# FFN-in units of a hybrid decoder layer: five pairs of weight tiles in seven-product form instead of four

## The chip, the core and the metric

The kernel runs on one core of a Trainium2 chip. The metric is the device time of one execution in microseconds (us), the median of three runs. Lower is better.

## What is computed

One decoder layer on 256 tokens of width 2048, in float32: x = x + 1/2 SwiGLU_1(RMSNorm(x)), then a token mixer (16 heads of 128, half dilated-window attention, half forgetting attention), then x = x + 1/2 SwiGLU_2(RMSNorm(x)). The change touches the first product of both SwiGLU blocks:

```python
D_FF = ((8 * D_MODEL // 3 + 127) // 128) * 128     # 5504

def swiglu_ffn(x, w_in, w_out):
    gate, up = jnp.split(x @ w_in, 2, axis=-1)
    return (jax.nn.silu(gate) * up) @ w_out
```

x is 256 x 2048 here, w_in is 2048 x 11008. With D_MODEL = 2048 the weights of both FFNs are most of what the kernel reads.

## The kernel before, in words

**Products.** Each float32 value is cut into a high and a low part, and a product of two tiles is three matmuls: high x high, high x low, low x high. ScalarE makes the high part of a weight tile (`whi`, helper `split` at L849), VectorE subtracts it to get the low part (`wlo`, L1188). A "half" is what one such split gives: up to 1024 elements per partition, two weight tiles of 128 x 512. `whi` and `wlo` have `SLOTS` = 4 slots each and halves are numbered through the whole program: half h goes to slot h % 4, ScalarE waits with `weights_used` until TensorE is through with half h - 4, VectorE waits for ScalarE (`weights_hi`), TensorE for VectorE (`weights_lo`).

**Units.** FFN-in is cut into 11 units of 512 columns of gate and of up (the last one has 384). Unit 0 is plain (`plain_unit`). Units 1 to 10 (`unit`, once per engine) do contraction tiles 0 to 7 plainly and tiles 8 to 15 in a seven-product form (after Strassen and Winograd). The four blocks of weights are B11 (tiles 8 to 11, up), B12 (8 to 11, gate), B21 (12 to 15, up) and B22 (12 to 15, gate); the two blocks of tokens stand for the rows. A form is a run of two halves, and each of the weight tiles in it is multiplied for one block of tokens only: 6 matmuls a half. A plain half is multiplied for both: 12 matmuls. The order, the same on all engines, is T1, B11, (turn of the activations of the unit before), G0 (two plain halves), T2, B21, T3, G1 (two), B22, T4, U0 and U1 (four): 22 halves. T1, T2, T3 and T4 are sums of weight blocks. T1 = B11 + B12 is made by VectorE in `tsum` (`sum_t1`, L1350), T3 = B12 + B22 in place of B12 (`sum_t3`, L1357), both at the end of the unit before. T2 and T4 are made in `tsum` by accumulating transfers that POOL issues (`add_piece`, L478).

**The order of VectorE inside a unit** is written out by hand (`unit` in the vector block): the low parts in the order above, and between them SwiGLU of the unit before (three steps, L1242 to L1248, behind B11's first half), the subtraction behind G1 (L1413), the add onto the gate inside T4 (L1419), the second subtraction behind the first half of U0 (L1424), `sum_t1` behind U1's first half and `sum_t3` behind its second. It waits in this order, strictly:

```python
split(base + B11, piece_half(n + LOAD["B11"], 0, w2), w2)
swiglu(u, j - 1)
split(base + B11 + 1, piece_half(n + LOAD["B11"], 1, w2), w2)
```

**Loads.** SP issues one transfer of 1 MB per weight piece into the six slots of `raw` (`piece`, L370), each behind a wait for the last use of its slot; the eight pieces of a unit go in one order (`LOAD`). x (2 MB) stays in SBUF all the time. It is needed for the squares of its norm and then when FFN-out's result is added to it (`join`, `x_update`).

Of the kernel before, what the change touches and what calls it, by code (L numbers as in the profile page):

```python
# [43 lines left out]
T1, B11, G0, T2, B21, T3, G1, B22, T4, U0, U1 = 0, 2, 4, 6, 8, 10, 12, 14, 16, 18, 20  # L44
UNIT_HALVES = 22

LOAD = {"B11": 0, "B12": 1, "B22": 2, "G0": 3, "B21": 4, "G1": 5, "U0": 6, "U1": 7}
# [61 lines left out]
OUT_P[0] = 8 * UNITS  # L109
# [3 lines left out]
OUT_P[1] = IN_P[1] + 8 * UNITS  # L113
# [14 lines left out]

def raw_slot(n):
    for u, end in ((0, QKV_P), (1, END_P)):  # L130
        if OUT_P[u] <= n < end:
            c, i = (n - OUT_P[u]) // ACT_PAIRS, (n - OUT_P[u]) % ACT_PAIRS
            q = OUT_LOADS[c][i] - 2 * OUT_GROUPS[c]
            return 3 + (2 * c * OUT_GROUPS[0] + OUT_LOADS[c][i]) % 3 if q < 0 else (c * ACT_PLAIN[0] + q) % 3
    for first, slots in ((IN_P[1], RAW_SLOTS), (QKV_P, QKV_RAW_SLOTS), (0, RAW_SLOTS)):
        if n >= first:
            return (n - first + (sum(ACT_PLAIN) if slots == QKV_RAW_SLOTS else 0)) % slots
# [3 lines left out]
for _n in range(END_P):  # L141
    RAW_FULL[_n] = 16 * (1 + sum(1 for _m in range(_n) if raw_slot(_m) == raw_slot(_n)))
# [11 lines left out]
def layer(nc, io, out):  # L154
# [3 lines left out]
    with ctx:  # L158
# [47 lines left out]
        place[0] = arena + 36 * 1024  # L206
        xg = sb("xg", [P, KT // 2, SEQ])
# [40 lines left out]
        rows_dram = nc.dram_tensor("forget_rows", (H_B, SEQ), f32).ap()  # L248
        scratch = nc.dram_tensor("bias_vectors", (P, H_A * VEC), f32).ap()
# [23 lines left out]
        raw_full = [sem(f"raw_full{s}") for s in range(RAW_SLOTS)]  # L273
# [49 lines left out]
        xg_ready, s_summed, s_hi, s_ready = (sem(n) for n in ("xg_ready", "s_summed", "s_hi", "s_ready"))  # L323
# [19 lines left out]
        def _(sp):  # L343
            def free(n):
                for u in range(2):
                    if IN_P[u] <= n < OUT_P[u]:
                        j, i = (n - IN_P[u]) // 8, (n - IN_P[u]) % 8
                        if j == 0:
                            return weights_lo, IN[u] + 2 * i + 2
                        if i == LOAD["B21"]:  # L350
                            return t4_added, 16 * ((UNITS - 1) * u + j)
                        last = {LOAD["B11"]: B11, LOAD["B21"]: B21, LOAD["B12"]: T3, LOAD["B22"]: B22, LOAD["G0"]: G0, LOAD["G1"]: G1, LOAD["U0"]: U0, LOAD["U1"]: U1}[i]
                        return weights_lo, unit_half(u, j) + last + 2
# [9 lines left out]

            def piece(n, src, tiles, w):
                slot = raw_slot(n)
                before = [m for m in range(n) if raw_slot(m) == slot]
                if before:
                    sem_free, value = free(before[-1])
                    sp.wait_ge(sem_free, value)
                sp.dma_start(raw[:, slot, 0:tiles * w].rearrange("p (k f) -> p k f", k=tiles), src).then_inc(raw_full[slot], 16)  # L370
# [8 lines left out]
            for u in range(2):  # L379
                w_in = io[f"ffn{u + 1}_w_in"][0].rearrange("(k p) f -> p k f", p=P)  # L380
                w_out = io[f"ffn{u + 1}_w_out"][0].rearrange("(t p) d -> p t d", p=P)
                for j in range(UNITS):
                    n, w = IN_P[u] + 8 * j, UNIT_W[j]
                    gate, up = slice(W * j, W * j + w), slice(D_FF + W * j, D_FF + W * j + w)
                    if j == 0:
# [23 lines left out]
                        for q in range(4):  # L409
                            piece(n + 4 + q, w_in[:, 4 * q:4 * q + 4, up], 4, w)  # L410
                            if u == 0 and q < 2:
                                for c in (2 * q, 2 * q + 1):
                                    sp.dma_start(x[:, :, c * W:(c + 1) * W], x_rows[:, :, c * W:(c + 1) * W]).then_inc(x_loaded[c], 16)
                    else:
                        piece(n + LOAD["B11"], w_in[:, 8:12, up], 4, w)
                        piece(n + LOAD["B12"], w_in[:, 8:12, gate], 4, w)
                        piece(n + LOAD["B22"], w_in[:, 12:16, gate], 4, w)
                        piece(n + LOAD["G0"], w_in[:, 0:4, gate], 4, w)
                        piece(n + LOAD["B21"], w_in[:, 12:16, up], 4, w)
                        piece(n + LOAD["G1"], w_in[:, 4:8, gate], 4, w)  # L420
                        piece(n + LOAD["U0"], w_in[:, 0:4, up], 4, w)
                        piece(n + LOAD["U1"], w_in[:, 4:8, up], 4, w)
# [27 lines left out]
        def _(pool):  # L450
# [22 lines left out]
            def add_piece(u, j, name, after, done):  # L473
                n, w = IN_P[u] + 8 * j, UNIT_W[j]
                k, col = {"B22": (12, W * j), "B21": (12, D_FF + W * j)}[name]
                pool.wait_ge(weights_lo, unit_half(u, j) + after + 2)
                pool.wait_ge(raw_full[raw_slot(n + LOAD[name])], RAW_FULL[n + LOAD[name]])
                pool.dma_start(tsum[:, 0:4 * w], raw[:, raw_slot(n + LOAD[name]), 0:4 * w], accum_op=ALU.add).then_inc(done, 16)  # L478

            for j in range(1, UNITS):  # L480
                add_piece(0, j, "B22", T1, t2_added)
                add_piece(0, j, "B21", T2, t4_added)
            pool.wait_ge(weights_lo, out_half(0, PASSES - 1, ("form", OUT_GROUPS[1] - 1, "T4")) + 1)
# [23 lines left out]
            x_power(2)  # L507
            for j in range(1, UNITS):
                add_piece(1, j, "B22", T1, t2_added)
                add_piece(1, j, "B21", T2, t4_added)  # L510

        @block.tensor
        def _(pe):
# [45 lines left out]
            def form(h, bank_out, stationary, w, start):  # L559
                for i in range(2):  # L560
                    pe.wait_ge(weights_lo, h + i + 1)
                    slot = (h + i) % SLOTS
                    for k in range(2):
# [4 lines left out]
                        last = mm(bank_out[:, 0:w], st_lo, hi, start=False, stop=i == 1 and k == 1, skip_group_check=True)  # L568
# [32 lines left out]
            def unit(u, j):  # L601
# [3 lines left out]
                if j == 1:  # L605
                    pe.wait_ge(silu_done, 2 * (UNITS * u + 1))
                    pe.wait_ge(s_ready, 4 * (u + 1))
                    if u == 0:
# [3 lines left out]
                form(base + T1, Z, lambda k, t: sf[:, 0, k, t, :], w, True)  # L612
                form(base + B11, Y, lambda k, t: xs[:, 8 + k, t, blk0], w, True)
                act_turn(u, j - 1)
                pe.wait_ge(copied, 3 * first + 1)
                for i in range(2):
                    plain(base + G0 + i, 2 * i, (Z, X), (False, True), w, -1)
                pe.wait_ge(copied, 3 * first + 2)
                form(base + T2, Y, lambda k, t: sf[:, 1, k, t, :], w, False)
                form(base + B21, V, lambda k, t: xs[:, 12 + k, t, blk0], w, True)  # L620
                pe.wait_ge(copied, 3 * first + 3)
                form(base + T3, Y, lambda k, t: sf[:, 2, k, t, :], w, False)
                for i in range(2):
                    plain(base + G1 + i, 4 + 2 * i, (Z, X), (False, False), w, 7)
                form(base + B22, Z, lambda k, t: sf[:, 3, k, t, :], w, False)
                pe.wait_ge(w_done, first + 1)
                form(base + T4, Y, lambda k, t: xs[:, 12 + k, t, blk1], w, False)
                for i in range(4):
                    plain(base + U0 + i, 2 * i, (V, Y), (False, False), w, 7)
# [210 lines left out]
        def _(act_e):  # L840
# [58 lines left out]
            def act_hi(u, c, k):  # L899
# [6 lines left out]
                else:  # L906
                    act_e.wait_ge(weights_used, unit_half(u, UNITS - 1) + B22 + 2)
                A(aw_hi[:, a, a_in, :], act[:, k, :], ACT.Copy).then_inc(aw_hi_ready, 1)

            def group_act_hi(u, c, g, part):  # L910
# [3 lines left out]
                else:  # L914
                    act_e.wait_ge(weights_used, unit_half(u, UNITS - 1) + B22 + 2)
# [22 lines left out]
            def plain_unit(u):  # L938
                w2 = 2 * UNIT_W[0]
                for i in range(2 * IN_HALVES):  # L940
# [32 lines left out]
                    if i == 13:  # L973
                        for f in range(4):
                            act_e.wait_ge(s_summed, 4 * u + (1, 3, 3, 4)[f])
                            A(sf[:, f, :, 0, :], s_sum(f), ACT.Copy).then_inc(s_hi, 1)
                    if i == 14:
                        silu(u, 0)

            def unit(u, j):  # L980
                Y, V, Z, X = unit_banks(j)
                base, n, w, s = unit_half(u, j), IN_P[u] + 8 * j, UNIT_W[j], j % 2
                first, w2 = (UNITS - 1) * u + j - 1, 2 * w
                act_e.wait_ge(sums_done, 2 * first + 1)
                for i in range(2):
                    split(base + T1 + i, tsum[:, i * w2:(i + 1) * w2], w2)
                loaded(n + LOAD["B11"])
                for i in range(2):
                    split(base + B11 + i, piece_half(n + LOAD["B11"], i, w2), w2)
                loaded(n + LOAD["G0"])  # L990
                split(base + G0, piece_half(n + LOAD["G0"], 0, w2), w2)
                act_e.wait_ge(weights_used, base + T1 + 2)
                A(gset[:, s, 1, 0:w], Z[:, 0:w], ACT.Copy).then_inc(copied, 1)
                split(base + G0 + 1, piece_half(n + LOAD["G0"], 1, w2), w2)
                act_e.wait_ge(weights_used, base + B11 + 2)
                act_e.wait_ge(act_f_done, 2 * (UNITS * u + j))
                A(p1s[:, 0:w], Y[:, 0:w], ACT.Copy).then_inc(copied, 1)
                act_e.wait_ge(t2_added, 16 * (first + 1))
                for i in range(2):
                    split(base + T2 + i, tsum[:, i * w2:(i + 1) * w2], w2)  # L1000
                loaded(n + LOAD["B21"])
                for i in range(2):
                    split(base + B21 + i, piece_half(n + LOAD["B21"], i, w2), w2)
                act_e.wait_ge(sums_done, 2 * first + 2)
                split(base + T3, piece_half(n + LOAD["B12"], 0, w2), w2)
                act_e.wait_ge(weights_used, base + T2 + 2)
                A(gset[:, s, 0, 0:w], Y[:, 0:w], ACT.Copy).then_inc(copied, 1)
                split(base + T3 + 1, piece_half(n + LOAD["B12"], 1, w2), w2)
# [675 lines left out]
```

## Time and profile before

| what | value |
|---|---|
| median of three runs | 1764.4 us (1764.1 to 1764.69) |
| the profiled execution's own time | 1763.82 us |
| its span, first to last instruction | 1762.0 us |
| TensorE busy | 1755.3 us (100%) |
| VectorE busy | 1408.5 us (80%) |
| ScalarE busy | 1074.9 us (61%) |
| read from HBM | 347 MB, 199 GB/s over the span |
| mean granted TensorE clock | 1.000 |

Busy time of TensorE is that of pipelined matmuls whose ends are modelled: a matmul of 512 columns is shown with 0.39 us, but the next one starts 0.23 us behind it. The starts give the pace. A small gap does not lower the busy time by its length.

### The profile page before, as it was taken

What the parts mean: (1) busy time and instruction counts of PE and PEld (TensorE: products, weight loads), DVE (VectorE), ACT (ScalarE), POOL (GpSimd) and SP (SyncE); (2) the same over time, 40 slices, a digit from 0 to 9 for tenths busy, and PEclk for the clock granted to TensorE, in tenths of its full rate; (3) what the DMA queues carried; (4) which work ended last, traced back from release to release, by engine and by line L of the source; (5) the groups of instructions that cost most, each with busy time, mean ns of one, the idle gap of its engine ahead of it and who ended that gap; (6) DMA issues with size and microseconds to landing.
All of it is one profiled execution on the core that took longest, in us unless ns stands there. A gap on an engine that the chain in (4) does not pass through costs nothing.

```text
span 1762.0 us, 20916 instructions
## 1 busy us (share of the span) xinstructions
PE 1755.3 (100%) x8036; PEld 1463.3 (83%) x8036; DVE 1408.5 (80%) x1587; ACT 1074.9 (61%) x1359; POOL 62.7 (4%) x74
## 2 busy tenths in 40 slices
PE   9999999999999999999999999999999999999999
PEld 7788888888988888888888888888888888988887
DVE  7888888887899998575655655888888888799998
ACT  7566666666666666554545544666666666666665
POOL 0000000000000001100000000000000000000000
PEclk9999999999999999999999999999999999999999
DMA  9888788876654556555455547687788887764762
GB/s 378 272 261 260 251 250 249 252 252 201 217 215 184 210 215 208 178 193 177 160 188 163 173 168 262 169 256 244 249 260 260 260 261 240 226 204 166 259 213 90
DMA packets 160691, 391.75 MB, mean 222 GB/s; under 512 B 6504, under 2 KB 15232, under 8 KB 155856
## 3 DMA queue, kind: packets, MB, share of 16 engines
q1 hardware_dynamic: 152288, 342.02, 54.7%
q0 software_dynamic: 7184, 46.42, 12.6%
q10 hardware_dynamic: 1120, 1.97, 0.3%
q8 instruction: 64, 1.05, 0.2%
q14 instruction: 35, 0.29, 0.0%
HBM read 347.37 MB, written 3.69 MB: 199 GB/s over the span
## 4 chain that ended last, share of the span: by engine, by line
PE 95%; DVE 2%; DMA 1%; SPq 1%; issue 1%; ACT 0%; POOL 0%; ACTq 0%; POOLq 0%; DVEq 0%
PE bank L584 9%; PE bank L582 9%; PE bank L583 9%; PE bank L566 7%; PE bank L568 7%; PE bank L567 7%; PE bank L523 7%; PE bank L525 7%; PE bank L524 6%; PE bank L653 5%; PE bank L655 5%; PE bank L654 5%; PE bank L679 3%; PE bank L681 3%; PE bank L680 3%; PE bank L551 1%
## 5 line engine op out<-in xcount | busy, mean ns | idle before, releaser
L1188 DVE TENSOR_TENSOR wlo<-raw,whi 128x1024 fp32r<-128x1024 f32 (+1 forms) x586 | 696.6, 1207 | 224.7 <-ACT whi L849 222.0
L849 ACT ACTIVATE whi<-raw 128x1024 fp32r<-128x1024 f32 (+1 forms) x586 | 611.0, 1047 | 390.2 <-PE bank L525 189.2
L582 PE MATMUL bank<-whi,xs 128*128 128x512 f32 (+1 forms) x768 | 297.9, 388 | 0.4 <-DVE xs L1370 0.2
L584 PE MATMUL bank<-whi,xs 128*128 128x512 f32 (+1 forms) x768 | 295.6, 385 | 0.0
L583 PE MATMUL bank<-wlo,xs 128*128 128x512 f32 (+1 forms) x768 | 295.5, 385 | 0.0
L1188 DVE TENSOR_TENSOR wlo<-tsum,whi 128x1024 fp32r<-128x1024 f32 (+1 forms) x120 | 140.2, 1196 | 60.5 <-ACT whi L849 60.5
L849 ACT ACTIVATE whi<-tsum 128x1024 fp32r<-128x1024 f32 (+1 forms) x120 | 122.2, 1036 | 103.9 <-PE bank L584 64.1
L582 PEld LDWEIGHTS bank<-whi,xs 128*128 128x128 f32 x768 | 144.4, 188 | 29.0 <-issue 0.9
L584 PEld LDWEIGHTS bank<-whi,xs 128*128 128x128 f32 x768 | 144.3, 188 | 27.7
L583 PEld LDWEIGHTS bank<-wlo,xs 128*128 128x128 f32 x768 | 144.4, 188 | 26.8
L653 PE MATMUL bank<-whi,aw_hi 128*128 128x512 f32 x420 | 164.0, 391 | 0.0
L655 PE MATMUL bank<-whi,aw_lo 128*128 128x512 f32 x420 | 163.5, 389 | 0.0
L654 PE MATMUL bank<-wlo,aw_hi 128*128 128x512 f32 x420 | 163.4, 389 | 0.0
L523 PE MATMUL bank<-whi,xs 128*128 128x512 f32 x384 | 155.1, 404 | 0.4 <-DVE wlo L1188 0.4
L525 PE MATMUL bank<-whi,xs 128*128 128x512 f32 x384 | 150.1, 391 | 0.0
L524 PE MATMUL bank<-wlo,xs 128*128 128x512 f32 x384 | 149.5, 389 | 0.0
L566 PE MATMUL bank<-whi,sf 128*128 128x512 f32 (+1 forms) x320 | 122.8, 384 | 1.0 <-DVE wlo L1188 1.0
L568 PE MATMUL bank<-whi,sf 128*128 128x512 f32 (+1 forms) x320 | 122.8, 384 | 0.0
L567 PE MATMUL bank<-wlo,sf 128*128 128x512 f32 (+1 forms) x320 | 122.7, 384 | 0.0
L1052 ACT ACTIVATE whi<-raw 128x1024 fp32r<-128x1024 f32 x80 | 84.8, 1060 | 61.8 <-PE bank L655 38.9
L1453 DVE TENSOR_TENSOR wlo<-raw,whi 128x1024 fp32r<-128x1024 f32 x80 | 97.2, 1221 | 1.7 <-ACT whi L1052 0.8
L653 PEld LDWEIGHTS bank<-whi,aw_hi 128*128 128x128 f32 x420 | 78.8, 188 | 17.4 <-issue 1.4
(203 smaller groups left out, 2670.4 us busy)
## 6 DMA issues: line engine op xcount, KB each, us to landing
raw<-ffn_w_in SPq DMA_DIRECT2D x158, 1024.0 KB, 7.1
raw<-ffn_w_out SPq DMA_DIRECT2D x84, 1024.0 KB, 6.5
raw<-w_in SPq DMA_DIRECT2D x48, 1024.0 KB, 5.1
tsum<-raw POOLq DMA_DIRECT2D x36, 1024.0 KB, 7.2
raw<-w_out SPq DMA_DIRECT2D x16, 1024.0 KB, 4.9
raw<-ffn_w_in SPq DMA_DIRECT2D x16, 768.0 KB, 4.6
tsum<-raw POOLq DMA_DIRECT2D x4, 768.0 KB, 5.7
x<-x SPq DMA_DIRECT2D x4, 512.0 KB, 12.4
```

Of the source, the lines that this page charges most:

```text
L523: mm(banks[b][:, 0:w], stationary[:, k, 0, tok], hi, start=k == 0, stop=False, skip_group_check=True)
L524: mm(banks[b][:, 0:w], stationary[:, k, 0, tok], lo, start=False, stop=False, skip_group_check=True)
L525: last = mm(banks[b][:, 0:w], stationary[:, k, 1, tok], hi, start=False, stop=k == k_total - 1, skip_group_check=True)
L566: mm(bank_out[:, 0:w], st_hi, hi, start=start and i == 0 and k == 0, stop=False, skip_group_check=True)
L582: mm(banks[b][:, 0:w], xs[:, k + i, 0, tok], hi, start=starts[b] and k + i == 0, stop=False, skip_group_check=True)
L583: mm(banks[b][:, 0:w], xs[:, k + i, 0, tok], lo, start=False, stop=False, skip_group_check=True)
L584: last = mm(banks[b][:, 0:w], xs[:, k + i, 1, tok], hi, start=False, stop=k + i == last_k, skip_group_check=True)
L653: mm(bank_out[:], st_hi, hi, start=i == 0, stop=False, skip_group_check=True)
L654: mm(bank_out[:], st_hi, lo, start=False, stop=False, skip_group_check=True)
L655: last = mm(bank_out[:], st_lo, hi, start=False, stop=k == FT - 1, skip_group_check=True)
L849: A(whi[:, h % SLOTS, 0:n_el], src, ACT.Copy).then_inc(weights_hi, 1)
L1188: V.tensor_tensor(wlo[:, h % SLOTS, 0:n_el], src, whi[:, h % SLOTS, 0:n_el].bitcast(f32), ALU.subtract).then_inc(weights_lo, 1)
```

## The change

Tiles 6 to 15 go through the seven-product form (five pairs) and tiles 0 to 5 are plain. Each form has three halves, of two, two and one weight tiles (15 matmuls), and the six plain halves are GA, GB, GC and UA, UB, UC. A unit has 27 halves. `SLOTS` stays 4. The fifth tile of each block (a "mini", 256 KB) is a transfer of its own, and so is its part of the accumulating transfers; VectorE's two sums get a second instruction of 512 elements each. The minis and one plain piece lie in SBUF where x was: in FFN 1 x is loaded for its squares and again behind the units, in FFN 2 POOL stores it to DRAM (`x_kept`) and loads it again. SP's queue waits in unit 1 for that (`ss_done`, `x_psum`, `x_stored`). There are five slots for form pieces and three for plain half pieces, and SP's order of loads is a new one. `sum_t3` moves from the end of the unit before to between GA and GB of its own unit; `sum_t1` of the next unit stands between UA and UB. The forms' token sums (`form_sums`) are of five tiles, with one more split (`last_form_split`).

```diff
-T1, B11, G0, T2, B21, T3, G1, B22, T4, U0, U1 = 0, 2, 4, 6, 8, 10, 12, 14, 16, 18, 20
-UNIT_HALVES = 22
+FORM_K0, FORM_PAIRS = 6, 5
+T1, B11, GA, GB, T2, B21, T3, GC, B22, T4, UA, UB, UC = 0, 3, 6, 7, 8, 11, 14, 17, 18, 21, 24, 25, 26
+UNIT_HALVES = 27
...
+            def form_piece(u, j, name):
...
+                wait_free(n)
+                sp.dma_start(raw[:, raw_slot(n), 0:4 * w].rearrange("p (k f) -> p k f", k=4),
+                             w_in[:, k:k + 4, col:col + w]).then_inc(raw_full[raw_slot(n)], 16)
+                if j == 1 and name == "B11":
+                    sp.wait_ge(ss_done, 8 * (2 * u + 1))
+                    if u:
+                        sp.wait_ge(x_psum, 8)
+                        sp.wait_ge(x_stored, 16)
+                sp.dma_start(minis[:, raw_slot(n), 0:w], w_in[:, k + 4, col:col + w]).then_inc(raw_full[raw_slot(n)], 16)
...
                     else:
+                        if j + 1 < UNITS:
+                            form_piece(u, j + 1, "B12")
+                        plain_piece(u, j, "UA")
+                        plain_piece(u, j, "UB")
+                        if j + 1 < UNITS:
+                            form_piece(u, j + 1, "B22")
+                        plain_piece(u, j, "UC")
+                        if j + 1 < UNITS:
+                            form_piece(u, j + 1, "B21")
+                            if j + 2 < UNITS:
+                                form_piece(u, j + 2, "B11")
+                            plain_piece(u, j + 1, "GA")
+                            plain_piece(u, j + 1, "GB")
+                            plain_piece(u, j + 1, "GC")
...
             def add_piece(u, j, name, after, done):
+                pool.dma_start(tsum[:, 0:4 * w], raw[:, raw_slot(n), 0:4 * w], accum_op=ALU.add).then_inc(done, 16)
+                pool.dma_start(tmini[:, 0:w], minis[:, raw_slot(n), 0:w], accum_op=ALU.add).then_inc(done, 16)
+
+            def x_again(u):
+                pool.wait_ge(weights_lo, OUT[u])
+                pool.dma_start(x[:], (x_kept if u else io["x"][0]).rearrange("(b p) d -> p b d", p=P)).then_inc(x_back, 16)
...
             def unit(u, j):
-                for i in range(2):
-                    split(base + T1 + i, tsum[:, i * w2:(i + 1) * w2], w2)
-                split(base + B11, piece_half(n + LOAD["B11"], 0, w2), w2)
+                for i in range(3):
+                    form_split(T1, i)
+                form_split(B11, 0, "B11")
                 swiglu(u, j - 1)
-                split(base + B11 + 1, piece_half(n + LOAD["B11"], 1, w2), w2)
-                split(base + G0, piece_half(n + LOAD["G0"], 0, w2), w2)
-                split(base + G0 + 1, piece_half(n + LOAD["G0"], 1, w2), w2)
+                for i in range(1, 3):
+                    form_split(B11, i, "B11")
+                plain_split("GA", GA)
+                sum_t3(u, j)
+                plain_split("GB", GB)
...
+                for i in range(3):
+                    form_split(B22, i, "B22")
+                form_split(T4, 0)
+                dve.wait_ge(weights_used, base + GC + 1)
                 dve.wait_ge(w_done, first + 1)
                 V.tensor_tensor(gset[:, s, 1, 0:w], X[:, 0:w], gset[:, s, 1, 0:w], ALU.add).then_inc(gate_added, 1)
-                split(base + T4 + 1, tsum[:, w2:2 * w2], w2)
-                split(base + U0, piece_half(n + LOAD["U0"], 0, w2), w2)
-                dve.wait_ge(weights_used, base + B22 + 2)
+                for i in range(1, 3):
+                    form_split(T4, i)
+                dve.wait_ge(weights_used, base + B22 + 3)
                 dve.wait_ge(copied, 3 * first + 3)
                 V.tensor_tensor(gset[:, s, 0, 0:w], Z[:, 0:w], gset[:, s, 0, 0:w], ALU.subtract).then_inc(gate_added, 1)
-                split(base + U0 + 1, piece_half(n + LOAD["U0"], 1, w2), w2)
-                split(base + U1, piece_half(n + LOAD["U1"], 0, w2), w2)
+                plain_split("UA", UA)
                 if j + 1 < UNITS:
                     sum_t1(u, j + 1)
-                split(base + U1 + 1, piece_half(n + LOAD["U1"], 1, w2), w2)
-                if j + 1 < UNITS:
-                    sum_t3(u, j + 1)
+                plain_split("UB", UB)
+                plain_split("UC", UC)
```

## Rows read from the trace of the kernel before

**Rows 1.** The page, parts 1 and 2: busy time of the engines, granted clock by slice.
```profile
PE 1755.3 (100%) x8036; PEld 1463.3 (83%) x8036; DVE 1408.5 (80%) x1587; ACT 1074.9 (61%) x1359; POOL 62.7 (4%) x74
...
PEclk9999999999999999999999999999999999999999
```

**Rows 2.** Waits of TensorE: engine and line, releaser, us in total, times, longest.
```profile
PE bank L531 <- POOL ident L455: 1.6, 1, 1.6
PE bank L566 <- DVE wlo L1188: 1.0, 1, 1.0
```

**Rows 3.** The chain that ended last: start, duration, work (turns of two steady units).
```profile
184.48 0.87 PE bank L551 x8
...
226.20 0.88 PE bank L551 x8
```

**Rows 4.** Timeline of TensorE: start, duration, line, operation; width 512, then 384.
```profile
159.83 0.39 PE L582 MATMUL bank<-whi,xs 128*128 128x512 f32 x1
...
178.87 0.39 PE L566 MATMUL bank<-whi,sf 128*128 128x512 f32 x1
...
434.95 0.33 PE L582 MATMUL bank<-whi,xs 128*128 128x384 f32 x1
...
446.91 0.33 PE L582 MATMUL bank<-whi,xs 128*128 128x384 f32 x1
```

**Rows 5.** Timeline of VectorE from T4's first half to B11's second half.
```profile
161.18 1.23 DVE L1188 TENSOR_TENSOR wlo<-tsum,whi 128x1024 fp32r<-128x1024 f32 x1 [0.91 <-ACT whi L849]
...
165.26 1.23 DVE L1188 TENSOR_TENSOR wlo<-raw,whi 128x1024 fp32r<-128x1024 f32 x1 [0.19 <-ACT whi L849]
166.40 0.68 DVE L1424 TENSOR_TENSOR gset<-bank,gset 128x512 f32<-128x512 f32 x1
167.00 2.35 DVE L1188 TENSOR_TENSOR wlo<-raw,whi 128x1024 fp32r<-128x1024 f32 x2
169.27 2.29 DVE L1350 TENSOR_TENSOR tsum<-raw 128x2048 f32<-128x2048 f32 x1
171.47 1.22 DVE L1188 TENSOR_TENSOR wlo<-raw,whi 128x1024 fp32r<-128x1024 f32 x1
...
177.50 1.23 DVE L1188 TENSOR_TENSOR wlo<-raw,whi 128x1024 fp32r<-128x1024 f32 x1 [0.33 <-ACT whi L849]
179.07 0.75 DVE L1242 SCALAR_TENSOR_TENSOR gset<-bank,rstd,gset 128x512 f32<-128x512 f32 x1 [0.34 <-PE bank L584]
...
181.12 3.49 DVE L1188 TENSOR_TENSOR wlo<-raw,whi 128x1024 fp32r<-128x1024 f32 x3
```

**Rows 6.** Timeline of ScalarE: two high parts that waited for TensorE.
```profile
160.09 1.06 ACT L849 ACTIVATE whi<-tsum 128x1024 fp32r<-128x1024 f32 x1 [0.75 <-PE bank L584]
...
179.07 1.07 ACT L849 ACTIVATE whi<-raw 128x1024 fp32r<-128x1024 f32 x1 [1.60 <-PE bank L584]
```

**Rows 7.** Timeline of VectorE: two adds of 512 elements back to back.
```profile
36.12 0.69 DVE L1212 TENSOR_TENSOR xg<-xg 128x512 f32<-128x512 f32 x1
36.73 0.68 DVE L1213 TENSOR_TENSOR xg<-xg 128x512 f32<-128x512 f32 x1
```

**Rows 8.** The one data stall: VectorE, TensorE, and 60 to 70 us with the clock 1.00.
```profile
64.10 2.36 DVE L1188 TENSOR_TENSOR wlo<-tsum,whi 128x1024 fp32r<-128x1024 f32 x2 [5.43 <-ACT whi L849]
...
65.47 0.47 PE L566 MATMUL bank<-whi,sf 128*128 128x512 f32 x1 [1.00 <-DVE wlo L1188]
65.78 0.40 PE L567 MATMUL bank<-wlo,sf 128*128 128x512 f32 x1
...
60.00:70.00 10.00, 9.00 (x40) 7.17 (x39) 5.77 (x5) 6.48 (x8) 0.87 (x1) 1.00 0.56 163
```

**Rows 9.** Timeline of VectorE: the sum for the unit of width 384.
```profile
419.53 1.75 DVE L1350 TENSOR_TENSOR tsum<-raw 128x1536 f32<-128x1536 f32 x1
421.20 1.22 DVE L1188 TENSOR_TENSOR wlo<-raw,whi 128x1024 fp32r<-128x1024 f32 x1
```

**Rows 10.** DMA issues: transfer, count, KB each, median us from issue to landing.
```profile
tsum<-raw POOLq DMA_DIRECT2D x36, 1024.0 KB, 7.2
...
tsum<-raw POOLq DMA_DIRECT2D x4, 768.0 KB, 5.7
```

More of the change, by code:

```diff
@@ L166, in sb @@
             return t
+        x_at = place[0]
         x = sb("x", [P, TB, D_MODEL])
+        x_end = place[0]
         xs_at = place[0]
@@ L346, in free @@
                     if IN_P[u] <= n < OUT_P[u]:
[L347 to L353, printed above, removed]
+                        if n < IN_P[u] + 8:
+                            return weights_lo, IN[u] + 2 * (n - IN_P[u]) + 2
+                        j, i = divmod(n - IN_P[u] - 8, UNIT_PIECES)
+                        last = (B11 + 2, T3 + 2, B22 + 2, T4, GA, GB, GC, UA, UB, UC)[i]
+                        return weights_lo, unit_half(u, j + 1) + last + 1
                     end = (QKV_P, END_P)[u]
@@ L362, in free, with wait_free @@
                 return weights_lo, QKV + 2 * (n - QKV_P) + 2
+            def wait_free(n):
+                slot = raw_slot(n)
+                shared = {RAW_SLOTS - 1: (RAW_SLOTS - 1, RAW_SLOTS, RAW_SLOTS + 1), RAW_SLOTS: (RAW_SLOTS - 1, RAW_SLOTS),
+                          RAW_SLOTS + 1: (RAW_SLOTS - 1, RAW_SLOTS + 1)}.get(slot, (slot,))
+                for t in shared:
+                    before = [m for m in range(n) if raw_slot(m) == t]
+                    if before:
+                        sem_free, value = free(before[-1])
+                        sp.wait_ge(sem_free, value)
@@ L364, in piece @@
             def piece(n, src, tiles, w):
                 slot = raw_slot(n)
[L366 to L369, printed above, removed]
+                wait_free(n)
                 sp.dma_start(raw[:, slot, 0:tiles * w].rearrange("p (k f) -> p k f", k=tiles), src).then_inc(raw_full[slot], 16)
@@ L473, in add_piece @@
             def add_piece(u, j, name, after, done):
[L474 to L478, printed above, removed]
+                n, w = unit_piece(u, j, name), UNIT_W[j]
+                pool.wait_ge(weights_lo, unit_half(u, j) + after + 3)
+                pool.wait_ge(raw_full[raw_slot(n)], RAW_FULL[n])
+                pool.dma_start(tsum[:, 0:4 * w], raw[:, raw_slot(n), 0:4 * w], accum_op=ALU.add).then_inc(done, 16)
[3 more added lines that the diff above has]
+                pool.dma_start(x[:], (x_kept if u else io["x"][0]).rearrange("(b p) d -> p b d", p=P)).then_inc(x_back, 16)
             for j in range(1, UNITS):
@@ L995, in unit @@
-                act_e.wait_ge(weights_used, base + B11 + 2)
+                plain_split("GB", GB)
+                act_e.wait_ge(weights_used, base + B11 + 3)
                 act_e.wait_ge(act_f_done, 2 * (UNITS * u + j))
                 A(p1s[:, 0:w], Y[:, 0:w], ACT.Copy).then_inc(copied, 1)
[L998 to L1001, printed above, removed]
@@ L1002, in unit @@
-                for i in range(2):
-                    split(base + B21 + i, piece_half(n + LOAD["B21"], i, w2), w2)
+                act_e.wait_ge(t2_added, 32 * (first + 1))
+                for i in range(3):
+                    form_split(T2, i)
+                loaded(unit_piece(u, j, "B21"))
+                for i in range(3):
+                    form_split(B21, i, "B21")
                 act_e.wait_ge(sums_done, 2 * first + 2)
-                split(base + T3, piece_half(n + LOAD["B12"], 0, w2), w2)
@@ L1006, in unit @@
-                act_e.wait_ge(weights_used, base + T2 + 2)
+                form_split(T3, 0, "B12")
+                act_e.wait_ge(weights_used, base + T2 + 3)
                 A(gset[:, s, 0, 0:w], Y[:, 0:w], ACT.Copy).then_inc(copied, 1)
-                split(base + T3 + 1, piece_half(n + LOAD["B12"], 1, w2), w2)
-                loaded(n + LOAD["G1"])
-                for i in range(2):
-                    split(base + G1 + i, piece_half(n + LOAD["G1"], i, w2), w2)
-                loaded(n + LOAD["B22"])
@@ L1013, in unit @@
-                for i in range(2):
-                    split(base + B22 + i, piece_half(n + LOAD["B22"], i, w2), w2)
-                act_copy(u, j - 1)
-                act_e.wait_ge(t4_added, 16 * (first + 1))
-                for i in range(2):
-                    split(base + T4 + i, tsum[:, i * w2:(i + 1) * w2], w2)
-                loaded(n + LOAD["U0"])
-                for i in range(2):
-                    split(base + U0 + i, piece_half(n + LOAD["U0"], i, w2), w2)
-                loaded(n + LOAD["U1"])
@@ L1023, in unit @@
-                split(base + U1, piece_half(n + LOAD["U1"], 0, w2), w2)
+                for i in range(1, 3):
+                    form_split(T3, i, "B12")
+                plain_split("GC", GC)
+                loaded(unit_piece(u, j, "B22"))
+                for i in range(3):
+                    form_split(B22, i, "B22")
+                act_copy(u, j - 1)
+                act_e.wait_ge(t4_added, 32 * (first + 1))
+                for i in range(3):
+                    form_split(T4, i)
+                plain_split("UA", UA)
@@ L1406, in unit, with form_split @@
-                split(base + B21 + 1, piece_half(n + LOAD["B21"], 1, w2), w2)
-                for i in range(2):
-                    split(base + T3 + i, piece_half(n + LOAD["B12"], i, w2), w2)
-                for i in range(2):
-                    split(base + G1 + i, piece_half(n + LOAD["G1"], i, w2), w2)
-                dve.wait_ge(weights_used, base + T3 + 2)
+                def form_split(form, i, name=None):
+                    src = form_half(unit_piece(u, j, name), i, w) if name else t_half(i, w)
+                    split(base + form + i, src, form_el(i, w))
@@ new lines, in plain_split @@
+                def plain_split(name, half):
+                    split(base + half, plain_half(unit_piece(u, j, name), w2), w2)
+                for i in range(3):
+                    form_split(T1, i)
+                form_split(B11, 0, "B11")
+                swiglu(u, j - 1)
+                for i in range(1, 3):
+                    form_split(B11, i, "B11")
+                plain_split("GA", GA)
+                sum_t3(u, j)
+                plain_split("GB", GB)
+                for i in range(3):
+                    form_split(T2, i)
@@ L1412, in unit @@
+                for i in range(3):
+                    form_split(B21, i, "B21")
+                for i in range(3):
+                    form_split(T3, i, "B12")
+                plain_split("GC", GC)
+                dve.wait_ge(weights_used, base + T3 + 3)
                 dve.wait_ge(copied, 3 * first + 1)
                 V.tensor_tensor(gset[:, s, 1, 0:w], gset[:, s, 1, 0:w], Y[:, 0:w], ALU.subtract).then_inc(w_done, 1)
-                for i in range(2):
-                    split(base + B22 + i, piece_half(n + LOAD["B22"], i, w2), w2)
```

199 lines of the change are left out of this document (129 added, 70 removed).

## The prediction, made before the changed kernel was built

> **What bounds the kernel now.** I read the totals and the slices first: TensorE is busy 1755.3 us of a span of 1762.0 at a granted clock of 9 tenths or more everywhere [rows 1]. The list of who waited for whom leaves TensorE only single waits; the longest on data is 1.00 us for one weight half [rows 2]. So every matmul taken out is time gained, as long as VectorE and ScalarE deliver the split weights as early as now. A steady FFN-in unit repeats every 41.72 us, from one turn of the activations to the next [rows 3]. Its 180 matmuls of 512 columns start 0.2267 us apart: 84 of them lie between the second half of G1 and the next unit's T1, 178.87 - 159.83 = 19.04 us [rows 4]. The turn takes the other 0.9.
>
> **What it removes.** A pair of weight tiles costs 24 matmuls in plain form and 21 in seven products. A unit goes from 7 x 12 + 8 x 12 = 180 to 7 x 15 + 6 x 12 = 177. There are 9 units of width 512 and one of 384 in each of the two FFNs: 54 matmuls at 0.2267 and 6 at 0.173 (11.96 us for the 69 between two starts at that width [rows 4]) are 12.2 + 1.0 = 13.3 us.
>
> **What it adds on VectorE.** Back to back a split of 1024 elements takes 1.14 us (165.26 to 166.40), a small add on a PSUM bank 0.60 (166.40 to 167.00), a sum of 2048 elements 2.20 (169.27 to 171.47), the three SwiGLU steps 2.05 (179.07 to 181.12) [rows 5]; 512 elements take 0.61 [rows 7]. Per unit before: 22 splits, two sums, some 3.8 us of small steps, 33.2 us in all. After: 20 full splits, 7 of 512 elements, two sums and two of 512 elements, 36.3 us. A unit without stalls would be 41.0 us, so VectorE still fits on average. What decides is the order inside the unit, because there are still only four slots for split weights: half h can be split by ScalarE only when TensorE has used half h-4, and VectorE takes its list strictly in turn.
>
> The handover costs, all seen before: a half used to ScalarE's start 0.26 (159.83 to 160.09) or 0.20 (178.87 to 179.07) us, its copy 1.06 [rows 4, 6]; VectorE then starts within 0.03; from its end to the matmul 0.13 us (the split of 64.10 ends at 65.34, the matmul starts at 65.47) [rows 8]. The first matmul after a stall is followed by the next one 0.31 us later, not 0.23, so a restart adds 0.08 [rows 8].
>
> **Place one: the second half of B11.** Now B11's first half is split at 177.50, before TensorE is through with the last unit, since its slot is freed by the last plain half but one; SwiGLU follows at 179.07 and the second half at 181.12 [rows 5], 0.5 us ahead of TensorE. After, T1 has three halves, so the slot of B11's first half is freed by UC, the very last half of the unit before. Count from its end, which is T1's start on TensorE. ScalarE 0.20 + 1.07, VectorE starts at 1.30, ends the first half at 2.44, SwiGLU (behind it in VectorE's list) at 4.49, the second half at 5.72; TensorE can go at 5.85. It wants it after 15 + 6 matmuls, at 4.76. **Stall 1.1 us.** T3's sum sits further on, between GA and GB: from B11's second half VectorE needs 0.61 + 1.14 + 2.81 + 1.14 = 5.70 us to GB's end, TensorE 9 matmuls, the turn and GA, 5.66. That is even, and worth 0 to 0.2 more.
>
> **Place two: UB.** Count from the end of GC, which frees T4's first slot. ScalarE 0.26 + 1.06, VectorE starts at 1.35 and from there is never idle: T4's first half 1.14, the add onto the gate 0.60, T4's other two 1.14 + 0.61, the subtraction 0.60, UA 1.14 (done at 6.6, wanted at 6.8), then the next unit's T1 sum 2.20 + 0.61, then UB 1.22: 10.6, plus 0.13 is 10.7. TensorE wants UB after B22, T4 and UA, 42 matmuls, at 9.5. **Stall 1.2 us.** Before, four plain halves stand here and two of them lie behind the sum as cover: it starts at 169.27 [rows 5] while TensorE has just begun the first. The two stalls add, for each starts again from a point of TensorE's own. Elsewhere in the forms I find about 0.8 us to spare: three halves of a form are 15 matmuls, 3.4 us, against 0.26 + 1.06 + 0.03 + 1.22 for one half's way.
>
> **The sum per FFN.** Place one: eight units (2 to 9) at 1.1 are 8.8. Unit 1 has two of the three SwiGLU steps: 0.5. Unit 10 has 384 columns: steps shrink to about 0.76 (a sum takes 1.67 us, 419.53 to 421.20, for 2.20 [rows 9]), but SwiGLU is still of width 512 and TensorE is through in 21 x 0.173 = 3.6 us: 1.4. Place two: eight at 1.2 are 9.6; unit 9 sums for the narrow unit, 0.5. The entry into unit 1 has one more split and wider form sums, about 1.8 us on VectorE, less the T3 sum that moved behind: 0.2. Together 21.0, for two FFNs 42.0. Restarts: 38 x 0.08 = 3.0. Net: -13.3 + 42.0 + 3.0 = +31.7 us.
>
> **The rest.** The accumulating transfers get a second, small one behind each. A transfer of 768 KB lands in 5.7 us and one of 1024 KB in 7.2 [rows 10], so I take 1.5 for 256 KB more: 8.7. The T1 halves are split about 1.2 us ahead of TensorE's end of the unit before, so T2's sum lands near 7.6 on the clock of place one, and ScalarE comes to it at 8.6: covered by 1 us there and by nearly 3 on TensorE. If it were uncovered the low bound is 0 and the high bound 1.5 a unit. In the very first unit the transfer is already late (the 1.00 us wait); I add 0.5, between 0 and 3. Loads per unit are the same bytes. SP's queue is held in FFN 1 until the squares of x are done and in FFN 2 until x is stored; behind it wait the rest of B11, B12, B22, GA, GB and B21 for unit 1, which are first used some 10 to 20 us later: 0, at most 3 each. Reloading x (2 MB) beside FFN-out's first weights: 0, since these now wait for form slots that come free early in the last unit; at most 3 each, and below zero nothing. Total +32.2 on the profiled execution's 1763.8, which is 0.6 under the median of 1764.4; on the median that gives 1796.6.
>
> **A rule against the change.** Across the 1.00 us wait the granted clock stayed at 1.00, its 2.4 GHz level, in the window around it [rows 8]. The Trainium skill (TensorE: Matmul & The Clock Gate, on oscillation) says that gaps in TensorE's work can bring the clock to the lower level. The row agrees with me for one gap; it is a rival below for two gaps a unit.
>
> **The rivals.** (1) VectorE keeps up after all, say because a handover is shorter or SwiGLU overlaps: only the matmuls count, 1764.4 - 13.3 = 1751. For it: the mean load, 36.3 of 41 us. Against: both chains above are made of steps seen back to back, and each would have to lose over 1 us. It would turn at 1.1 us in one place. Chance 0.09. (2) One of the two places is real and the other not: 1764.4 - 13.3 + 0.5 + about 21 + 1.5 = 1774. Chance 0.08. (3) The clock falls to its 1.2 GHz level in the stalls: if one form's 15 matmuls ran at half pace in each of 20 units, 20 x 3.4 = 68 us more, 1865. Chance 0.02. (4) T2's sum or the loads come last: 20 x 1.5 us more, 1827. For it: transfers of five parts where there were four, and plain weights now have three small slots. Against: the margins above. Chance 0.04. The forecast, both stalls: 0.77.
>
> **The numbers.** About 0.2% is what a measurement of this kernel can tell from no change, so 3.5 us. Faster than that: rival 1, 0.09. Within: a single small stall a unit, 0.03, taken from rival 2. Slower: the rest, 0.88. Two stalls a unit with 0.3 us of error each are 11 us; with the bounds of the rest the range goes from 1778 to 1812, and leaves out rivals 1 and 3 and most of 2 and 4.
>
> **What would show it.** In the changed kernel's profile the list of waits should show TensorE waiting for VectorE's split weights some 38 times in its form line and its plain line, about 20 us each; a turn should come every 43.5 us instead of 41.72; VectorE should show no idle time from T4's first half to UB. Wrong would be: an unbroken TensorE in the units (rival 1), ScalarE waiting for the accumulating transfer (rival 4), a granted clock below 1.00 (rival 3).

## The result and the profile after

The changed kernel takes 1814.3 us (1813.04 to 1814.99) against 1764.25 us, a ratio of 1.0283 with a 95% interval of 1.0265 to 1.0301: 50.0 us slower where I forecast 32.2, and 2.3 us above the top of my range. The direction and the steady unit were forecast; the start of the second FFN was not.

The page, parts 1 and 2, and the head of part 6, answer to [rows 1] and [rows 10]:

```profile
span 1811.2 us, 21336 instructions
...
PE 1759.3 (97%) x7976; PEld 1449.1 (80%) x7976; DVE 1467.6 (81%) x1729; ACT 1113.4 (61%) x1461; POOL 100.1 (6%) x117
...
PEclk9999999999999999999999999899999999999999
...
tsum<-raw POOLq DMA_DIRECT2D x36, 1024.0 KB, 6.9
```

60 matmuls are gone (8036 to 7976), and yet TensorE's span is longer. Its list of waits, beside [rows 2] (engine and line, releaser, us in total, times, longest):

```profile
PE bank L669 <- DVE wlo L1300: 29.9, 22, 8.1
PE bank L685 <- DVE wlo L1300: 15.3, 19, 0.9
```

L669 is the matmul of a form, L685 that of a plain half. Some 20 waits of 0.9 us stand in either, and among the first group there are long ones. The steady unit shows where the short ones are. POOL issues the accumulating transfer for T2 once a unit, at a fixed place; here are two of them:

```profile
186.48 0.86 POOL L572 DMA_DIRECT2D tsum<-raw  x1 [26.32 <-DVE wlo L1300]
...
230.00 0.86 POOL L572 DMA_DIRECT2D tsum<-raw  x1 [26.30 <-DVE wlo L1300]
```

43.52 us apart, where it was 41.72 [rows 3] and where I said 43.5. VectorE's timeline over one of these units, beside [rows 5]:

```profile
215.99 1.23 DVE L1300 TENSOR_TENSOR wlo<-tsum,whi 128x1024 fp32r<-128x1024 f32 x1 [0.31 <-ACT whi L953]
217.13 0.68 DVE L1546 TENSOR_TENSOR gset<-bank,gset 128x512 f32<-128x512 f32 x1
217.73 1.22 DVE L1300 TENSOR_TENSOR wlo<-tsum,whi 128x1024 fp32r<-128x1024 f32 x1
218.86 0.68 DVE L1300 TENSOR_TENSOR wlo<-tmini,whi 128x512 fp32r<-128x512 f32 x1
219.46 0.68 DVE L1551 TENSOR_TENSOR gset<-bank,gset 128x512 f32<-128x512 f32 x1
220.06 1.21 DVE L1300 TENSOR_TENSOR wlo<-raw,whi 128x1024 fp32r<-128x1024 f32 x1
221.20 2.28 DVE L1466 TENSOR_TENSOR tsum<-raw 128x2048 f32<-128x2048 f32 x1
223.40 0.68 DVE L1467 TENSOR_TENSOR tmini<-minis 128x512 f32<-128x512 f32 x1
224.00 1.22 DVE L1300 TENSOR_TENSOR wlo<-raw,whi 128x1024 fp32r<-128x1024 f32 x1
...
232.22 1.23 DVE L1300 TENSOR_TENSOR wlo<-raw,whi 128x1024 fp32r<-128x1024 f32 x1 [2.51 <-ACT whi L953]
233.36 0.74 DVE L1359 SCALAR_TENSOR_TENSOR gset<-bank,rstd,gset 128x512 f32<-128x512 f32 x1
...
235.41 1.22 DVE L1300 TENSOR_TENSOR wlo<-raw,whi 128x1024 fp32r<-128x1024 f32 x1
```

TensorE beside it:

```profile
225.27 0.50 PE L685 MATMUL bank<-whi,xs 128*128 128x512 f32 x1 [0.92 <-DVE wlo L1300]
...
230.87 0.39 PE L669 MATMUL bank<-whi,sf 128*128 128x512 f32 x1
...
236.68 0.50 PE L669 MATMUL bank<-whi,xs 128*128 128x512 f32 x1 [0.89 <-DVE wlo L1300]
```

The first block has no idle time from 215.99 on. UB's low part ends at 225.22 and TensorE begins at 225.27. UA began at 221.43, so UB was wanted 12 matmuls later, at 224.15: 1.1 us late. T1 begins at 230.87; B11's second half comes 5.81 us behind it, at 236.68, where 21 matmuls are 4.76: 1.05 us late. My two chains gave 1.2 and 1.1. Both waits are listed with only 0.9 us, since the matmul before them is drawn out to 0.39 us by its modelled end: the starts are to be compared, not the idle time.

What I had not seen is at unit 1 of FFN 2. The chain that ended last, from there (start, us, what):

```profile
1132.11 0.82 DVE xg L1328
...
1134.18 0.18 DVE xms L1343
...
1134.43 1.56 POOL rstd L559
1135.99 6.74 DMA x_kept<-x
...
1142.80 0.34 SPq L437
...
1143.66 5.18 DMA minis<-ffn_w_in
...
1148.93 2.29 DVE tsum L1466
...
1156.84 12.29 DMA tmini<-minis
```

And TensorE at its end, with the stretches around it (last three columns: granted clock, DMA share, GB/s):

```profile
1145.85 0.39 PE L687 MATMUL bank<-whi,xs 128*128 128x512 f32 x1
1154.32 0.77 PE L669 MATMUL bank<-whi,sf 128*128 128x512 f32 x1 [8.08 <-DVE wlo L1300]
...
1155.31 0.63 PE L671 MATMUL bank<-whi,sf 128*128 128x512 f32 x1
1155.74 0.63 PE L669 MATMUL bank<-whi,sf 128*128 128x512 f32 x1
```
```profile
1125.00:1135.00 10.00, 10.00 (x46) 8.29 (x45) 9.20 (x10) 6.14 (x9) 0.57 (x1) 1.00 0.01 2
...
1145.00:1155.00 10.00, 1.92 (x8) 1.31 (x7) 4.95 (x4) 3.14 (x4) 0.00 (x0) 0.69 1.05 402
1155.00:1165.00 10.00, 10.00 (x42) 8.14 (x41) 8.91 (x10) 5.11 (x7) 1.83 (x2) 0.80 1.06 324
```

Read from the top: VectorE's statistics of the norm (`xms`), POOL's rstd, and only then the store of x. In POOL's program the store stands behind `x_power(2)`. SP waits for the store before it loads B11's mini and everything behind it, and from 1125 to 1135 the DMA engines move 2 GB/s. B12's weights, the last that the T1 sum needs, then land at 1148.8, TensorE idles 8.1 us, and for some matmuls it starts one every 0.43 us instead of 0.23: the 1.2 GHz level. The last line shown is T2's sum: with the held loads all under way at once it lands 12.3 us after its issue, and TensorE waits another 1.7 us for it at 1171.62.

The two profiled executions are 49.2 us apart (spans of 1762.0 and 1811.2). POOL's first rstd of the mixer, a marker between the FFNs, stands at 709.71 us in the kernel before and at 729.43 in this one. So FFN 1 lost 19.7 us (I had 16.1) and the rest of the kernel, in the main FFN 2, lost 29.5 (16.1).

### The profile page after: what moved, and what is told of

Same layout as the page of the kernel before. It is cut to its first block, busy times and chain, and to the rows that moved or that the text cites. A ratio compares the mean times of both kernels' runs of the same rounds, so it can differ in the third digit from the quotient of the medians.

```text
span 1811.2 us, 21336 instructions
## 1 busy us (share of the span) xinstructions
PE 1759.3 (97%) x7976; PEld 1449.1 (80%) x7976; DVE 1467.6 (81%) x1729; ACT 1113.4 (61%) x1461; POOL 100.1 (6%) x117
## 3 DMA queue, kind: packets, MB, share of 16 engines
q8 instruction: 64, 1.05, 0.2%
## 4 chain that ended last, share of the span: by engine, by line
PE 76%; DVE 13%; issue 4%; DMA 3%; ACT 3%; SPq 1%; POOL 0%; ACTq 0%; DVEq 0%
PE bank L626 6%; PE bank L628 6%; PE bank L627 6%; DVE wlo L1300 6%; PE bank L685 5%; PE bank L687 5%; PE bank L686 5%; PE bank L757 5%; PE bank L759 5%; PE bank L758 5%; PE bank L669 5%; PE bank L670 5%; PE bank L671 5%; PE bank L783 3%; PE bank L785 3%
## 5 line engine op out<-in xcount | busy, mean ns | idle before, releaser
L1300 DVE TENSOR_TENSOR wlo<-raw,whi 128x1024 fp32r<-128x1024 f32 (+1 forms) x506 | 608.7, 1208 | 238.7 <-ACT whi L953 234.7
L953 ACT ACTIVATE whi<-raw 128x1024 fp32r<-128x1024 f32 (+1 forms) x506 | 530.0, 1049 | 340.0 <-PE bank L628 183.9
L685 PE MATMUL bank<-whi,xs 128*128 128x512 f32 (+1 forms) x608 | 239.2, 393 | 16.6 <-DVE wlo L1300 15.3
L687 PE MATMUL bank<-whi,xs 128*128 128x512 f32 (+1 forms) x608 | 234.7, 386 | 0.0
L686 PE MATMUL bank<-wlo,xs 128*128 128x512 f32 (+1 forms) x608 | 234.6, 386 | 0.0
L669 PE MATMUL bank<-whi,xs 128*128 128x512 f32 (+1 forms) x380 | 148.0, 390 | 16.9 <-DVE wlo L1300 16.9
L685 PEld LDWEIGHTS bank<-whi,xs 128*128 128x128 f32 x608 | 114.1, 188 | 50.8 <-DVE wlo L1300 27.3
L670 PE MATMUL bank<-wlo,xs 128*128 128x512 f32 (+1 forms) x380 | 146.1, 385 | 0.0
L671 PE MATMUL bank<-whi,xs 128*128 128x512 f32 (+1 forms) x380 | 146.0, 384 | 0.0
L669 PE MATMUL bank<-whi,sf 128*128 128x512 f32 (+1 forms) x320 | 124.7, 390 | 13.0 <-DVE wlo L1300 13.0
L687 PEld LDWEIGHTS bank<-whi,xs 128*128 128x128 f32 x608 | 114.2, 188 | 22.9
L686 PEld LDWEIGHTS bank<-wlo,xs 128*128 128x128 f32 x608 | 114.3, 188 | 19.7
```

The lines of the kernel that those rows point to most:

```text
L669: mm(bank_out[:, 0:w], st_hi, hi, start=start and i == 0 and k == 0, stop=False, skip_group_check=True)
L670: mm(bank_out[:, 0:w], st_hi, lo, start=False, stop=False, skip_group_check=True)
L685: mm(banks[b][:, 0:w], xs[:, k + i, 0, tok], hi, start=starts[b] and k + i == 0, stop=False, skip_group_check=True)
L686: mm(banks[b][:, 0:w], xs[:, k + i, 0, tok], lo, start=False, stop=False, skip_group_check=True)
L687: last = mm(banks[b][:, 0:w], xs[:, k + i, 1, tok], hi, start=False, stop=k + i == last_k, skip_group_check=True)
L953: A(whi[:, h % SLOTS, 0:n_el], src, ACT.Copy).then_inc(weights_hi, 1)
```

## The experiments

Each was timed beside the kernel before, on the same chip. The changed kernel itself was timed apart from them, so a gain against its 1814.3 us is good to some 3 us, going by the intervals.

| run | edit | us | ratio to before, 95% interval |
|---|---|---|---|
| e1_swiglu_first | SwiGLU ahead of B11 | 1797.0 | 1.0184 (1.0168 to 1.0199) |
| e2_t1_behind_ub | T1's sum behind UB | 1793.8 | 1.0165 (1.0149 to 1.0180) |
| e3_store_first | x stored ahead of rstd | 1799.9 | 1.0203 (1.0188 to 1.0218) |
| e4_t3_only | kernel before, T3's sum moved | 1764.4 | 1.0002 (0.9992 to 1.0011) |
| e7_three | e1 + e2 + e3 | 1764.9 | 1.0002 (0.9993 to 1.0011) |
| e5_three_and_bias | e7, bias vectors later | 1760.2 | 0.9978 (0.9970 to 0.9987) |
| e6_before_bias | kernel before, bias vectors later | 1764.6 | 1.0000 (0.9991 to 1.0009) |
| e8_b11_between | e5, B11 inside SwiGLU | 1757.65 | 0.9960 (0.9946 to 0.9974) |
| e9_wait_behind | e8, ahead of the wait | 1756.4 | 0.9958 (0.9945 to 0.9972) |

**Place one.** The first of the two orders on VectorE, one part of it undone:

```diff
-                form_split(B11, 0, "B11")
                 swiglu(u, j - 1)
-                for i in range(1, 3):
+                for i in range(3):
                     form_split(B11, i, "B11")
```

> The changed kernel with SwiGLU ahead of B11's first half on VectorE. Theory (VectorE's order costs 1.1 us at B11's second half): from T1's start on TensorE SwiGLU ends at 2.25, B11's first half at 3.5, its second at 4.6, so that 0.2 us of stall is left at the first half; about 18 small gains of 0.9 us, 1814.3 - 16 to 18 = 1797 us, and TensorE's waits in the form line fall by about 17 us. Rival (loads or transfers set the unit's length): no change, 1814.

Measured 1797.0 (1793.76 to 1799.0), 17.3 us less than the changed kernel. T2's transfer is issued every 42.56 us (185.41 to 227.97), 0.96 less than before the edit. The rival, the loads, has no share in that: this edit touches none. TensorE's form line, which had 22 waits, keeps 7, the long one among them:

```profile
PE bank L669 <- DVE wlo L1300: 15.2, 7, 8.2
```

**Place two.** `sum_t1` between UB and UC instead of between UA and UB.

> The changed kernel with the next unit's T1 sum behind UB instead of ahead of it on VectorE. Theory (the sum makes UB late by 1.2 us): UB is done at 7.8 where it is wanted at 9.5, UC at 11.9 where it is wanted at 12.2, so 17 gains of 1.2 us: 1814.3 - 19 to 21 = 1794 us, waits in the plain line fall from 15 us to under 3. Rival (loads): no change, 1814. Second rival (the stall only moves to UC): 1810.

Measured 1793.8, 20.5 us less. TensorE's list of waits no longer has the line L685 <- DVE wlo at all, while its form line stays:

```profile
PE bank L669 <- DVE wlo L1300: 29.5, 22, 8.2
```

**The store.** POOL's two statements for x_kept go ahead of `x_power(2)`.

> The changed kernel with POOL storing x ahead of its rstd instruction for FFN 2. Theory (the store sits behind an instruction that waits for the norm's sums, SP waits for the store, and unit 1's weights come 8 us late): the store starts near 1105 instead of 1136, the 8.1 us stall at the start of unit 1 and the clock's dip go, and 1814.3 - 10 to 13 = 1803 us. Rival (unit 1 of FFN 2 is late by its own work on VectorE): under 2 us gained, 1813.

Measured 1799.9, 14.4 us less, some more than I expected. The store is issued at 1104.43 and its 8.1 us wait is gone:

```profile
1104.43 0.75 POOL L608 DMA_DIRECT2D x_kept<-x  x1 [117.86 <-DVE x L1350]
...
1132.96 1.61 POOL L559 TENSOR_TENSOR rstd<-xms,neg_half 128x2 f32<-128x2 f32 x1 [27.77 <-DVE xms L1343]
```

Over 1145 to 1165 us its granted clock stays at 1.00. The two profiled executions are 13.5 us apart, and they can be compared transfer by transfer. At the marker between the FFNs 1.5 us are gained already, where this edit changes nothing (below, at the first unit of FFN 1). At T2's issue in unit 1 of FFN 2 it is 9.8 us (1156.22 against 1146.47), at T4's 13.2 (1173.50 against 1160.27), and so it stays to the last unit. The late store thus cost 11.8 us: 8.3 before T2's issue, which is the stall, and 3.5 behind it, where the changed kernel has the clock of 0.80 and the wait of 1.7 us for T2's sum. That sum lands 8.8 us after its issue here.

**T3's sum alone**, in the kernel before, between the two G0 halves:

> The kernel before with only T3's sum moved, to between the two G0 halves of its own unit. Theory: VectorE has 1.5 us idle there and 0.9 us of lead, so nothing changes within 0.1%: 1764. Rival (the moved sum itself makes the unit longer, by making the second G0 half late): 0.5 us a unit or more, 1774.

1764.4: in the kernel before, this move costs nothing. In the changed kernel the sum has its second instruction besides; there e2_t1_behind_ub bears on it, where TensorE waits for the low part of no plain half, GB's among them.

**All three.**

> The changed kernel with all three of these moved: SwiGLU ahead of B11, T1's sum behind UB, the store of x ahead of POOL's rstd. Theory (three separate costs): the gains of the single runs add, 17.3 + 20.5 + 14.4 = 52.2, 1814.3 - 52.2 = 1762 us, and a steady unit repeats every 41.3 us or less where the kernel before has 41.72. Rival (freed of one wait, the units run into T2's accumulating transfer or the loads, which then come last): half of it, 1775 to 1790, with ScalarE waiting for tmini.

1764.9, for 1762.1 by the sum of the single gains (17.3 + 20.5 + 14.4 = 52.2): they add to within 3 us, which is what the times can tell, so they are separate costs. It is level with the kernel before, not 13 us faster. In the steady units the list of TensorE's waits is empty, but they repeat every 41.35 us (T2's transfer at 181.83 and 223.18), where 177 matmuls and the turn are 41.0. And unit 1 of FFN 1 still has a stall of 3.3 us with a clock of 0.86 behind it.

**That first unit.** On POOL's queue the 1.5 MB transfer of the bias vectors is issued at 50.13, and T2's two at 54.00 and 54.58.

```diff
-            pool.dma_start(scratch, vec_dram.to_broadcast([P, H_A * VEC])).then_inc(vec_copied, 16)
...
                 add_piece(0, j, "B21", T2, t4_added)
+                if j == 1:
+                    pool.dma_start(scratch, vec_dram.to_broadcast([P, H_A * VEC])).then_inc(vec_copied, 16)
```

> The same with one more move: the 1.5 MB transfer of the bias vectors on POOL's queue goes behind the two accumulating transfers of FFN 1's unit 1. Theory (T2's sum of that unit lands 12.3 us after its issue because it stands behind this transfer and the loads): it lands in 8 to 10 us, the 3.2 us stall and the clock's dip behind it shrink by 2 to 4 us, 1759. Rival (the loads of SP alone make it late): no change, 1762.

> The kernel before with only the bias vectors' transfer moved behind the accumulating transfers of unit 1. Theory: its one data stall of 1.0 us goes, 1763.4 against 1764.5. Rival: no change.

With the three other moves: 1760.2, 4.7 us less than e7_three. T2's small transfer lands 8.8 us after its issue instead of 12.5. In the kernel before: no difference (1764.6 to 1764.45), as the rival said. Its wait of 1.0 us at 65.47 is gone, but two others have come, 0.4 us at 94.97 and 1.0 us at 100.33. The same two stretches in e7_three, then in e5_three_and_bias:

```profile
60.00:70.00 10.00, 6.69 (x33) 5.43 (x31) 4.80 (x5) 3.46 (x5) 0.00 (x0) 0.97 1.02 309
70.00:80.00 10.00, 10.00 (x39) 8.11 (x38) 7.87 (x9) 6.82 (x9) 1.73 (x2) 0.86 0.70 146
```
```profile
60.00:70.00 10.00, 10.00 (x49) 8.12 (x48) 8.10 (x8) 5.88 (x7) 1.85 (x3) 1.00 0.97 288
70.00:80.00 10.00, 10.00 (x46) 8.28 (x45) 8.36 (x10) 8.27 (x11) 0.44 (x1) 1.00 1.02 252
```

72 matmuls against 95 in 20 us (some of the latter are the short ones of the turn). The late transfer cost the stall and a piece of slow clock behind it. Whether the clock falls there is not the same in every run. TensorE waits 2.7 us for this sum in e1_swiglu_first and 2.9 in e3_store_first, and the 5 us behind it read:

```profile
70.00:75.00 5.00, 4.65 (x14) 3.77 (x15) 4.30 (x5) 2.86 (x4) 1.73 (x2) 0.69 0.47 119
```
```profile
70.00:75.00 5.00, 5.00 (x24) 4.14 (x23) 4.72 (x6) 3.97 (x6) 1.73 (x2) 1.00 0.62 143
```

The changed kernel fell there too (3.2 us, 0.66 over the same 5 us). Eight of its matmuls there start 0.43 us behind the one before instead of 0.23, 1.6 us in all, and that is the 1.5 us by which e3_store_first was ahead at the marker: luck, and no part of what the store cost.

**The last 0.35 us of a unit.** VectorE takes SwiGLU's three steps, then B11's first half, just 0.2 us too late. The first half goes between the second and the third step:

> The four moves, and B11's first half on VectorE between the second and the third step of SwiGLU. Theory: with SwiGLU wholly ahead the first half is ready 0.2 us late in each unit (a unit repeats every 41.35 us where 177 matmuls and the turn are 41.0); between the steps it is done at 2.75 and the second half at 4.6, both before they are wanted, a unit takes 41.05 us, and 18 x 0.3 = 5 us go: 1755. Rival (the units are held by something else, T2's sum or the turn): no change, 1760.

1757.65, half of what I wanted. VectorE's timeline shows that the first half now idles for the wait that belongs to the third step.

```profile
179.37 0.68 DVE L1363 TENSOR_TENSOR p1s<-bank,p1s 128x512 f32<-128x512 f32 x1
180.28 1.23 DVE L1301 TENSOR_TENSOR wlo<-raw,whi 128x1024 fp32r<-128x1024 f32 x1 [0.23 <-DVE p1s L1363]
181.42 0.74 DVE L1368 SCALAR_TENSOR_TENSOR gset<-p1s,rstd,gset 128x512 f32<-128x512 f32 x1
```

> As the version with B11's first half between the steps of SwiGLU, but ahead of VectorE's wait for the second step's result, which idled it for 0.23 us. Theory (B11's second half is just late by that): 18 gains of about 0.2 us, 1757.65 - 3 to 4 = 1754. Rival (some units are now held by the landing of T2's sum, which the idle 0.23 us only covers): under 1 us gained, 1757.

1756.4, 1.2 us less with overlapping intervals. The turns in the profiles show that my theory of that idle time was wrong. From turn to turn a steady unit of FFN 2 takes 41.35 us in e5_three_and_bias and 41.14 in e8_b11_between, 0.2 less where I had said 0.3, and taking the idle time out brings it to 41.12: 0.02 us a unit, not 0.2. The rest of the difference lies in FFN 1, where unit 2 of e8_b11_between took 41.83 us between its turns (102.36 to 144.19) and 41.19 in e9_wait_behind (101.63 to 142.82). Why is open.

Of the 13.3 us that the matmuls are worth this version shows 7.8 against the kernel before. I made no run for the other 5.5, but the profiles say where some of it lies. From the last turn of FFN 2 to the end it takes 221.84 us (1531.96 to 1753.8) for 219.69, 2.2 more with the same matmuls. ScalarE waits there once for 4.3 us, until 1532.74, for weights of FFN-out, while POOL's reload of x (2 MB, 12.5 us to landing) is under way, and VectorE, busy 97% of the next 50 us, has no room to catch up; that this is the reason is argued, not shown. In FFN 1 the same stretch, to the mixer, is not longer. About 1 us is that a unit gained 0.62 us (T2's transfer at 218.17 and 259.27, 41.10 for 41.72) and not 0.68. TensorE's own waits tell little of it: behind the first 11 us the longest is 0.4. ScalarE still waits 9.6 us in all, in six places from 150 to 440 us, for T2's sum without TensorE being late for it.

## Why the prediction was right and where it was wrong

- **Removed matmuls**: 60 fewer, as counted. Their worth was not seen alone; the mended version shows a unit of 41.10 us for 41.72, 0.6 us, and 0.68 was the sum.
- **Place one and place two**: right in place, cause and size (1.05 and 1.1 us a unit for 1.1 and 1.2), and right that they add; e1_swiglu_first and e2_t1_behind_ub each took one away. The period of 43.5 us came out to 0.02.
- **T3's sum**: right, free, in the kernel before by e4_t3_only; in the changed one no wait shows at it.
- **VectorE's load**: 20 x 1.14, 7 x 0.61, the sums and the small steps come to 36.5 us and not to 36.3. Nothing hangs on it.
- **The accumulating pairs**: in the steady units the second transfer lands 8.0 us after its own issue by the median between 180 and 400 us, 8.5 us after the first one's; I had 8.7. No stall, as said. In unit 1 of FFN 1 I booked 0.5 and at most 3 us: the stall is 3.2 and brings the slow clock, 3.6 us over my sum for that FFN, and the reason was the bias vectors' 1.5 MB on the same queue, which I had not looked for: moving them gave 4.7 us (e5_three_and_bias).
- **Reloading x**: booked at 0, at most 3 each. In FFN 1 it shows nothing. In FFN 2 the stretch behind the last turn is 1.6 us longer (1589.94 to 1811.2, 221.26 for 219.69). That the reload is the reason no run shows.
- **The step that failed**: "SP's queue is held in FFN 1 until the squares of x are done and in FFN 2 until x is stored ...: 0, at most 3 each". In FFN 2 it cost 11.8 us by the profiled pair; the 14.4 of the medians can hold a share of FFN 1's clock. The 11.8 and the 1.6 us above make up the 13.4 us by which FFN 2 lies over my sum, and without the 11.8 the time would have been inside the range. I asked when x is ready (it could have been stored at 1104.43, as e3_store_first shows) and not when POOL comes to the store. POOL is a queue in program order, and ahead of the store stands an rstd that needs statistics 30 us later. Then everything behind SP's wait was late together, B11's mini and B12 first, which the T1 sum needs at once, and not 10 to 20 us later as I had written. I had named the queue behind SP, but not the one ahead of POOL.
- **Rival 3**, the clock: wrong where I put it, for the stalls of 1.1 us left the clock at 1.00 in all steady units. Right in kind: after the waits of 3.2 and 8.1 us it fell. The Trainium skill (TensorE: Matmul & The Clock Gate, on oscillation) says that long gaps do this. The traces agree for those two waits and for the ones of 1.1 us, which did nothing; waits of 2.7 to 2.9 us went both ways.
- **Rivals 1, 2 and 4** fall: both places were real, and no transfer came last in a steady unit. In unit 1 of both FFNs T2's transfer did come last.

## What to carry to other kernels

Where an engine works through a hand-written order and buffers are few, its mean load says little: follow one chain from the event that frees a buffer, add every instruction that stands in between, and compare with the consumer's time to the same point. A wait added to a load queue is as late as the whole queue of the engine that signals it, so read that engine's program upwards from the signal and ask what each instruction there waits for. And a saving at the bound is only had once those orders are rewritten for it: here three moves were worth 49 us, nearly four times what the change itself could give.

## What the runs showed of the hardware

A wait of 1.1 us twice in 43 us left the granted clock at 1.00. A wait of 8.1 us was followed by matmuls of 512 columns starting 0.43 us apart, the 1.2 GHz level, and the stretch of 10 us from the start of which TensorE worked again had 0.80. After a wait of 3.3 us (e7_three) the next 10 us had 0.86 and 39 matmuls for 46. Of three waits at the same place, 2.7 us was followed by 0.69 over 5 us (e1_swiglu_first), 2.8 and 2.9 us by 1.00 (e2_t1_behind_ub, e3_store_first).

Two accumulating transfers issued one behind the other, 1 MB and 256 KB, landed 8.0 us after the second's issue in steady units (the 1 MB alone 7.2 before), but 12.3 us after it in unit 1 of both FFNs. In FFN 1 1.5 MB stood ahead of them on the same queue, and without these it was 8.8 (e5_three_and_bias). In FFN 2 nothing stood ahead of them, but SP's held loads filled the DMA engines, and with the loads in time it was again 8.8 (e3_store_first).
